# The last expert rows of a two-layer encoder, gathered into sixteen buffers in place of eight

## The reference, cut to what matters

```
for l in range(2):
    x = x + g1 * (mixers(h) @ w_out[l])
    h = rms_norm(x, norm2_g[l]) * (1.0 + sc2) + sh2
    # PEER: for each token 128 experts e (8 heads x 16) with gates g
    act = gelu(einsum('tkd,td->tk', peer_u[e], h))      # peer_u[e]: "up-rows" of 1024 f32
    y   = einsum('tk,tkd->td', g * act, peer_v[e])      # peer_v[e]: "down-rows" of 1024 f32
    x = x + g2 * y
return rms_norm(x, final_g)
```

## Time and profile before

| | us |
|---|---|
| median of 3 runs | 3650.46 |
| the profiled execution | 3636.02 |
| its span, first to last instruction | 3634.2 |
| POOL busy | 2283.0 |
| DVE busy | 2227.8 |
| PE busy | 1836.1 |
| gathers (q0), share of 16 DMA engines | 78.2% |

### The profile page before, as it was taken

The page is one execution under the profiler, slowest core; times in us unless marked ns, Lnnn a source line. Parts: engine busy times, 40 slices in busy tenths (PEclk is TensorE's granted clock), DMA queues, the critical chain, the costliest instruction groups (busy, mean ns, idle before and its releaser), DMA issues.

```text
span 3634.2 us, 30323 instructions
## 1 busy us (share of the span) xinstructions
PE 1836.1 (51%) x10176; PEld 894.3 (25%) x10176; DVE 2227.8 (61%) x5807; ACT 250.6 (7%) x683; POOL 2283.0 (63%) x2067
## 2 busy tenths in 40 slices
PE   6825452736454562566636455465636465233333
PEld 4425230513132230231304122232304122000000
DVE  6267757675768557765486746676585856645420
ACT  1200100001000100101000010001000110000000
POOL 0015667677667667555666766777676776767653
PEclk9767575767677776776758677676857676555666
DMA  6547899999999999999999999999999999999996
GB/s 247 211 158 267 302 409 342 357 369 390 379 352 368 337 406 364 407 415 405 382 375 374 349 360 396 343 378 361 398 370 366 358 370 412 361 362 378 361 344 232
DMA packets 314671, 1282.62 MB, mean 353 GB/s; under 512 B 34955, under 2 KB 35211, under 8 KB 303507
## 3 DMA queue, kind: packets, MB, share of 16 engines
q0 software_dynamic: 294912, 1073.87, 78.2%
q1 hardware_dynamic: 18740, 201.83, 13.7%
q10 hardware_dynamic: 864, 4.99, 0.4%
HBM read 1272.16 MB, written 8.39 MB: 352 GB/s over the span
## 4 chain that ended last, share of the span: by engine, by line
POOL 31%; PE 18%; DVE 16%; DMA 16%; issue 14%; another core or an unknown queue 5%; ACT 1%; SPq 0%; POOLq 0%; DVEq 0%; ACTq 0%
POOL ringV L236 18%; POOL ringU L226 13%; DMA ringV<-in_peer_v,idxP 9%; PE py L479 6%; DVE ringU L803 5%; DMA ringU<-in_peer_u,idx_g 5%; PE pj L551 4%; DMA ringU<-in_peer_u,idx_w 2%; PE pj L718 1%; PE pj L622 1%; PE pj L494 1%; PE pj L558 1%; PE pw L692 1%; PE pw L519 1%
## 5 line engine op out<-in xcount | busy, mean ns | idle before, releaser
L803 DVE CUSTOM_DVE_ANT_0 ringU<-ringU,h2g 128x1024 f32<-128x1024 f32 x1024 | 1224.6, 1225 | 800.0 <-DMA ringU<-in_peer_u,idx_g 549.7
L236 POOL DMA_INDIRECT ringV<-in_peer_v,idxP x1024 | 1144.6, 1118 | 581.4 <-issue 272.3
L479 PE MATMUL py<-ringV,wm 128*32 128x512 f32 x4096 | 817.8, 914 | 1125.2 <-DMA ringV<-in_peer_v,idxP 924.8
L226 POOL DMA_INDIRECT ringU<-in_peer_u,idx_g x960 | 1071.4, 1116 | 472.1 <-issue 284.2
L479 PEld LDWEIGHTS py<-ringV,wm 128*32 128x32 f32 x4096 | 160.3, 145 | 1646.9 <-issue 1575.9
L551 PE MATMUL pj<-hT,wring 128*128 128x128 f32 (+1 forms) x2560 | 329.8, 292 | 26.7 <-issue 18.8
L551 PEld LDWEIGHTS pj<-hT,wring 128*128 128x128 f32 (+1 forms) x2560 | 317.4, 201 | 63.3 <-issue 50.7
L226 POOL DMA_INDIRECT ringU<-in_peer_u,idx_w x64 | 62.2, 971 | 269.4 <-DVE gate_w L1299 246.1
L692 PE MATMUL pw<-hT,ckv_all 128*128 128x128 f32 x320 | 78.9, 401 | 94.1 <-issue 60.7
L718 PE MATMUL pj<-wring,mixT 128*128 128x512 f32 x256 | 118.3, 622 | 9.1 <-issue 8.4
L494 PE MATMUL pj<-ident,wk 128*128 128x128 f32 x168 | 43.5, 364 | 138.6 <-DVE wk L1165 61.3
(11 more groups left out here) (294 smaller groups left out, 1893.0 us busy)
## 6 DMA issues: line engine op xcount, KB each, us to landing
wring<-in_w_in SPq DMA_DIRECT2D x28, 2048.0 KB
wring<-in_w_mod SPq DMA_DIRECT2D x24, 2048.0 KB
wring<-in_w_out SPq DMA_DIRECT2D x16, 2048.0 KB
wring<-in_peer_w_q SPq DMA_DIRECT2D x16, 2048.0 KB
ringV<-in_peer_v,idxP POOLq DMA_INDIRECT x1024
ringU<-in_peer_u,idx_g POOLq DMA_INDIRECT x960
wring<-in_w_in SPq DMA_DIRECT2D x8, 784.0 KB
x_mix<-xs SPq DMA_DIRECT2D x8, 512.0 KB
```

The lines of the kernel that those rows point to most:

```text
L226: pool.indirect_dma_start(out=ringU[k % NR][:, :], out_offset=None, in_=ux, in_offset=bass.IndirectOffsetOnAxis(ap=idx[:, k:k + 1], axis=0 ...
L236: pool.indirect_dma_start(out=ringV[r % NR][:, :], out_offset=None, in_=vx, in_offset=bass.IndirectOffsetOnAxis(ap=idx[:, at:at + 1], axis=0),
L479: mm = t.matmul(py[32 * j:32 * j + 32, c * 512:(c + 1) * 512], wm[e % 2][:, at:at + 32], ringV[(4 * m + j) % NR][:, c * 512:(c + 1) * 512] ...
L803: v.tensor_tensor_reduce(out=ringU[k % NR][:, :], in0=ringU[k % NR][:, :], in1=h2g[:, :], scale=1.0, scalar=0.0, op0=ALU.mult, op1=ALU.add ...
```

## The change

It concerns only the last leg and the end of leg 8, where no up-rows are left to gather and `ringU` is empty. Rows 8 to 15 of the last leg, and from there on every second run of eight, go to `ringU` with the landing semaphores `landU`; the others stay in `ringV`. A new helper `fetch_tail` does this: it issues the same gather as `fetch_v`, with the same index columns, into buffer r % 16. At the end of leg 8 POOL issues, behind the rows 0 to 7 of before, the rows 8 to 15, each behind a wait for the dot that used its buffer, and all this ahead of POOL's arrival at the barrier. In the last leg POOL starts with row 16, and waits for `mixed` at r-15 in place of r-7. `down_row` tells PE for each row which buffer, which semaphore and which count. The number of gathers, their bytes, the matmuls and their order are the same.

```diff
+                def fetch_tail(r):
+                    m, j = divmod(r, 4)
+                    at = HE + HS * j + m
+                    q = r % (2 * NR)
+                    pool.indirect_dma_start(
+                        out=(ringV[q] if q < NR else ringU[q - NR])[:, :], out_offset=None, in_=vx,
+                        in_offset=bass.IndirectOffsetOnAxis(ap=idxP[(2 * NB) % 2][:, at:at + 1], axis=0),
+                    ).then_inc(landV[q] if q < NR else landU[q - NR], 16)
...
-                    if v_ is not None and r0 < HE:
+                    if u is None and v_ is not None and 2 * NR <= r0 < HE:
+                        for r in range(r0, r0 + 4):
+                            pool.wait_ge(S["mixed"], r - 2 * NR + 1)
+                            fetch_tail(r)
+                    if u is not None and v_ is not None and r0 < HE:
                         for r in range(r0, r0 + 4):
                             pool.wait_ge(S["mixed"], r - NR + 1)
                             fetch_v(r, idxP[(g - 1) % 2], 1)
...
                     for r in range(NR):
                         pool.wait_ge(S["mixed"], T - NR + r + 1 - off)
                         fetch_v(r, idxP[g % 2], 1)
+                    if not mixers:
+                        for r in range(NR, 2 * NR):
+                            pool.wait_ge(S["dots"], HK - 2 * NR + r + 1)
+                            fetch_tail(r)
                     pool.wait_ge(S["dots"], HK)
...
+                def down_row(r):
+
+                    if u is None and r % (2 * NR) >= NR:
+                        return ringU[r % NR], landU[r % NR], LANDU * 2 * NB + 16 * (r // (2 * NR) + 1)
+                    if u is None:
+                        return ringV[r % NR], landV[r % NR], landed + 16 * (r // (2 * NR) + 1)
+                    return ringV[r % NR], landV[r % NR], landed + 16 * (r // NR + 1)
...
                         for j in range(4):
-                            r = 4 * m + j
-                            t.wait_ge(landV[r % NR], landed + 16 * (r // NR + 1))
+                            _, land, count = down_row(4 * m + j)
+                            t.wait_ge(land, count)
...
-                                              ringV[(4 * m + j) % NR][:, c * 512:(c + 1) * 512],
+                                              down_row(4 * m + j)[0][:, c * 512:(c + 1) * 512],
```

## The result

Twelve runs of each kernel: before 3650.46 us (3632.31 to 3669.83), after 3630.32 us (3622.06 to 3651.72). The ratio is 0.995, with an interval of [0.9929, 0.9972]. That is 20.1 us by the medians, where 16.2 were forecast, and the time lies in the range. The interval goes from 10 to 26 us of gain, so it does not tell 16 from 20. The profiled execution took 3631.41 us, its span is 3629.6 us, 4.6 less than before's, at a mean granted clock of 0.688.

What follows compares the result with a forecast made beforehand. The last leg was taken as bound by its eight-buffer ring's round trip; 62 x 1.413 + 3.5 = 91.1 us in place of 107.3 gains 16.2, so 3650.46 - 16.2 = 3634.3 us, range 3627 to 3642.

Steps and rivals of the forecast that it cites:

- The ring stops being the bound; the DMA engines are next: Last leg: sixteen buffers allow 0.86 us a row, below the DMA engines' 1.413 and POOL's 1.24.
- 62 rows' worth at leg 8's rate and 3.5 us: Last leg, row 4's issue to last landing: 62 x 1.413 + 3.5 = 91.1 us instead of 107.3, gain 16.2.
- the Trainium skill's 358 GB/s: Last leg: a core's effective memory share; by it 1.46 us a row, 94.3 us, gain 13.0; not taken as a limit.
- The barrier costs nothing: Before the last leg: POOL arrives near 3508.0, not 3504.1, but row 16 has 6.6 us of cover; cost 0.
- POOL's waits follow the DMA engines' pace, gathers stay at 0.94: Last leg: POOL's waits for PE shrink to waits at the DMA's pace; each gather still takes 0.94 us.
- the third rival: Last leg: POOL becomes the bound at 2.26 us a row, 140 us, 33 us slower, 3683 us; chance 0.03.
- PE's last group as now: End of the last leg: PE's last group still ends 3.73 us behind the last landing.
- The first: Last leg: DMA share rises but rate stays between 304 and 335 GB/s; middle gain 4, 3646.5 us; chance 0.08.
- The second: Last leg: rate follows POOL's pace, 400 GB/s or more, 84.1 us, gain 23, 3627 us; chance 0.13.
- The fourth: Last leg: row 16 waits for the barrier or PE; 3 us less gain; no chance of its own.

Runs made afterwards that it cites:

- the wide kernel: Kernel after, with sixteen buffers for leg 8's down-rows and twenty-four in the last leg; run twice: 3527.33 us (0.9883 of before) and 3536.99 us (0.9903).
- the two other sets: Follow-up runs on two other chips, leg 8 at 406 to 413 GB/s; kernel after unchanged: 3545.53 us (0.9932 of before) and 3542.80 us (0.9921).

## Why the prediction was right, point by point

**The ring stops being the bound; the DMA engines are next.** Right for the ring: in the profiled pair the tail falls by 18.7 us, and the DMA engines' share in it rises from 0.86 to 0.98. That the DMA engines are next is shown where no count is late: there the tail has one length with 12, 16 and 24 buffers, and shrinks to POOL's pace when each row is half as long. In the pair's own kind it is not separated from POOL's pauses: 59 steps of 1.24 us, 8.8 us of pauses beyond the usual gap and 6.4 us for the last landing come to 88.4 us as well.

**The size: 62 rows' worth at leg 8's rate and 3.5 us.** The forecast was 91.1 us, measured 88.5. The term that was mis-sized is the rate: (88.5 - 3.5) / 62 = 1.371 us a row in place of 1.413. Leg 8 was taken for a stretch in which the DMA engines are the bound, and its own row says otherwise: POOL's 182.04 us with 182 gaps of 0.30 leave 23.4 of the 260 us idle. Between the dips the same gathers run at 410 GB/s, 1.28 us a row, as in the stretch from 3540 to 3545, where PE's groups start 5.1 us apart (3537.22, 3542.34, 3547.46) and not 5.6. What keeps the tail above 1.28 are for the most part patches like that from 3570 to 3575 (0.75, 265 GB/s), and they stand behind pauses of POOL that the prediction did not have. So that the sum came within 3 us is partly luck: leg 8's average already contained dips of the kind that the tail then had. In the executions without them the tail is 85.1 us. Of the Trainium skill's 358 GB/s (HBM Reference, Specifications (TRN2)) nothing was felt as a limit: 374 GB/s over 87 us here, 413 over 270 us of leg 8 in the wide kernel.

**The barrier costs nothing.** Right, and even its price was set too high. I had POOL arrive 3.8 us after row 4's start; it arrives before it (3520.0 against 3520.13), and PE's first group follows row 4 by 1.82 us, before by 1.72. The failing step was the reading of the earlier trace rows: I took the 3.9 us between lines 267 and 272 for the time that POOL's sequencer needs for twelve gathers. But it had all twelve handed over before the first began (3520.0), and with twenty it arrived with twelve left. The barrier from leg 7 to leg 8 does not explain the 3.9 us either, since it was open 2.3 us before line 272 passed: SP's load, which stands behind it, goes at 3136.28.

```profile
3136.28 0.52 SPq L1368 DMA_DIRECT2D wk<-x_mix  x1
```

What POOL waits for there is open.

**POOL's waits follow the DMA engines' pace, gathers stay at 0.94.** The gathers do (933 to 941 ns); the third rival, with 1.96 us each, is out. The waits do not follow the pace. POOL issues sixteen and more without a break and then sits idle for 3.5 us, and the reason isn't PE. Two groups of PE, one gather of POOL and one step of ACT, from the timeline of the kernel after:

```profile
3537.22 1.92 PE L504 MATMUL py<-ringU,wm 128*32 128x512 f32 x16 [1.61 <-DMA ringU<-in_peer_v,idxP]
...
3542.34 3.50 PE L504 MATMUL py<-ringU,wm 128*32 128x512 f32 x16 [3.19 <-DMA ringU<-in_peer_v,idxP]
...
3548.20 0.94 POOL L237 DMA_INDIRECT ringU<-in_peer_v,idxP  x1 [3.55 <-remote]
...
3548.89 0.49 ACT L313 ACTIVATE wm<-wTb 64x16 f32<-64x16 f32 x2 [26.59 <-remote]
```

The gather at 3548.20 is that of row 24; it needs nine rows mixed, and the group at 3537.22, with rows 8 to 11, was through at 3539.14. ACT's step needs sixteen; that group ended at 3545.84. The counts reached POOL 9 us and ACT 3 us after the work, the two at nearly one moment. The same pauses stand ahead of rows 40 and 56, which go out at 3571.21 and 3593.51. Patches of low share lie at these two (0.75 from 3570 to 3575, 0.93 from 3595 to 3600), but none at the first, where the share stays at 1.03 from 3544 to 3549. In the last leg of before, where POOL waits every four rows, they came at once: in the earlier trace rows PE's group ends at 3519.93 and POOL goes on at 3520.16. In the runs at 406 GB/s and more no wait of the whole trace bears the name "remote". The difference of the tails, 88.7 - 85.1 = 3.6 us, is what the slower kind of execution costs in the tail, late counts and patches together. Why they come late was argued in several ways and settled by no run.

**PE's last group as now.** 2.02 in place of 3.73 us, by the clock, which stood at its upper level (1.00); a matter of the single execution.

**The rivals.** The first (less rate, gain 4) is out. The second (400 GB/s and more, 84.1 us) has come true in its numbers in the two other sets: 405 to 415 GB/s inside the tail (3455 to 3515 us), and 85.1 us with sixteen buffers. Its reason did not: leg 8 runs at 406 to 413 there with DVE's dot products beside it, and POOL's pace is not what the tail follows, as the last row's 11.6 us to its landing show. The gain was 22.6 and 32.5 us there by the medians (the intervals go from 16 to 33 and from 17 to 39); the tail of the kernel before was not profiled at that rate. The fourth is out: row 16 waits neither for the barrier nor for PE.

## What to carry to other kernels

When two engines wait for each other over a ring, divide the round trip by the number of buffers, and the next slower resource gives the new pace; read its rate from a stretch of the same kernel in which it is the bound. A share of 0.97 over 260 us did not prove that here: look also whether the engine that issues the transfers ever stands idle in the stretch, and cut it into short pieces, since an average hides dips. Past the point where the ring covers it, more buffers bring nothing there (12, 16 and 24 gave one time where no count was late; where counts are late only 8 and 16 were tried), but they may bring something one stage earlier. A test that halves a load must halve only that: look at the busy share beside the time before believing it.

## What the runs showed of the hardware that I had not expected

- One program in two kinds of execution: 369 to 373 GB/s over the 270 us of leg 8 in some sets of runs, 406 to 413 in others, and 2% of the whole time between them (3637 to 3650 against 3568 to 3575 us). Both run at 410 in stretches, and the slower kind has pauses of POOL with dips to 189 to 320 GB/s beside them.
- A gather of 4-KB rows into 64 partitions took as long as one into 128: 208 GB/s at a share of 0.89, packets of 313 ns against 159.
- POOL's sequencer ran twelve gathers ahead of the engine; with twenty, the barrier behind them opened with the start of the ninth.
- Counts from PE reached POOL and ACT up to 9 us late while POOL issued without a break, in all runs at 370 GB/s and in none at 406 or more.
- The kernel's end, from the output's issue to the last instruction, took 11.3 us in the kernel after and 7.1 in the wide one; POOL's closing DRAIN took 8.15 and 3.90 of them.
